# Norm weights applied as per-partition scalars after the turn instead of as rows before it, in three norms of a two-block transformer kernel

## The reference

```python
def rms_norm(x, g):
    return x * rsqrt(mean(x * x, axis=-1) + EPS) * g

# first block
h = rms_norm(x, norm_mix);  x = x + mixer(h) @ w_out
h = rms_norm(x, norm_ffn)                                   # "norm2" in the kernel
x = x + (silu(h @ w_gate) * (h @ w_up)) @ w_down
x = rms_norm(x, final_norm)
# second block
h = rms_norm_2(x, ln_mix_g_2)                               # with final_norm: "norm3"
x = x + mixer_2(h @ w_in_2) @ w_out_2
h = rms_norm_2(x, ln_ffn_g_2)                               # "norm4"
# h @ w_query -> scores -> for each token 8 heads x 16 experts of 16384:
#   x += softmax(best) * gelu(expert_u[e] . h) * expert_v[e]
```

## Time and profile before

| what | value |
|---|---|
| time, median of 3 runs | 1166.69 us (1164.12 to 1166.91) |
| the profiled execution: its own time | 1164.98 us |
| its span in the trace | 1163.2 us |
| PE busy | 1046.1 us (90%) |
| DVE busy | 791.0 us (68%) |
| ACT busy | 610.7 us (52%) |
| POOL busy | 356.0 us (31%) |
| read from HBM | 367.82 MB |
| TensorE clock granted, mean | 0.987 of full speed |

### The profile page before, as it was taken

One profiled execution on the slowest core, in us unless ns is written; L12 is line 12 of the kernel. 1 busy time (PEld: TensorE's weight loads), 2 busy tenths in 40 slices (PEclk: granted clock), 3 DMA queues, 4 the chain that ended last, 5 costly groups with the idle time before them and its releaser, 6 DMA issues.

```text
span 1163.2 us, 13131 instructions
## 1 busy us (share of the span) xinstructions
PE 1046.1 (90%) x3786; PEld 649.8 (56%) x3786; DVE 791.0 (68%) x1694; ACT 610.7 (52%) x1343; POOL 356.0 (31%) x283
## 2 busy tenths in 40 slices
PE   8999999999999999999999898878787778877777
PEld 7788888888888877885554444323232223322222
DVE  5764666755545688879686876676676667667755
ACT  7565564544445467746655555535444543544453
POOL 1000000000000000024554544556455565556442
PEclk9999999999999999999999999999899999999999
DMA  9464357775535755679999999999999999999996
GB/s 327 160 202 130 124 177 232 269 217 180 182 106 181 253 183 179 229 252 419 421 420 423 421 421 421 421 421 421 422 419 419 423 421 416 422 421 422 423 421 282
DMA packets 95760, 369.49 MB, mean 318 GB/s; under 512 B 6544, under 2 KB 30104, under 8 KB 63072
## 3 DMA queue, kind: packets, MB, share of 16 engines
q0 software_dynamic: 38464, 273.46, 56.8%
q1 hardware_dynamic: 57248, 95.45, 24.9%
HBM read 367.82 MB, written 1.06 MB: 317 GB/s over the span
## 4 chain that ended last, share of the span: by engine, by line
PE 48%; DMA 22%; DVE 10%; ACT 8%; issue 7%; POOL 4%; SPq 1%; POOLq 0%; DVEq 0%; ACTq 0%
DMA uv_ring<-in_peer_uv,expert 21%; PE gemm L1746 11%; PE gemm L1748 11%; PE gemm L1747 11%; PE gemm L2159 11%; POOL uv_ring L481 4%; DVE uv_ring L1632 2%; DVE w_both L988 1%; ACT L940 1%; ACT L912 1%; ACT diag L946 1%; PE trb L1740 1%; ACT wgt L943 1%; ACT hid_g L940 1%; DMA x_sb<-in_x 1%
## 5 line engine op out<-in xcount | busy, mean ns | idle before, releaser
L2159 PE MATMUL gemm<-uv_ring,diag 128*128 128x512 f32 x1020 | 493.6, 621 | 102.8 <-ACT diag L946 102.3
L481 POOL DMA_INDIRECT uv_ring<-in_peer_uv,expert x256 | 344.6, 1346 | 355.3 <-PE gemm L2159 195.5
L1632 DVE CUSTOM_DVE_ANT_0 uv_ring<-uv_ring,gains_xT 128x1024 f32<-128x1024 f32 x256 | 312.2, 1224 | 172.6 <-DMA uv_ring<-in_peer_uv,expert 172.4
L2159 PEld LDWEIGHTS gemm<-uv_ring,diag 128*128 128x128 f32 x1020 | 185.0, 194 | 385.1 <-ACT diag L946 225.2
L988 DVE TENSOR_TENSOR w_both<-raw,w_both 128x1024 fp32r<-128x1024 f32 (+1 forms) x184 | 192.9, 1061 | 144.1 <-ACT w_both L534 143.4
L534 ACT ACTIVATE w_both<-raw 128x1024 fp32r<-128x1024 f32 (+1 forms) x184 | 168.7, 929 | 173.2 <-PE gemm L1748 170.4
L1747 PE MATMUL gemm<-w_both,hT_hi 128*128 128x512 f32 (+1 forms) x592 | 227.4, 384 | 0.0
L940 ACT ACTIVATE hid_g<-hid,scales 128x1 f32<-128x1 f32 x256 | 75.0, 293 | 280.8 <-DVE hid L1632 279.9
L1746 PE MATMUL gemm<-w_both,hT_hi 128*128 128x512 f32 (+1 forms) x544 | 215.8, 397 | 6.0 <-DVE w_both L988 5.8
L1748 PE MATMUL gemm<-w_both,hT_lo 128*128 128x512 f32 (+1 forms) x544 | 208.9, 384 | 0.0
L1747 PEld LDWEIGHTS gemm<-w_both,hT_hi 128*128 128x128 f32 x592 | 111.5, 188 | 26.2 <-issue 6.7
(11 more groups left out here) (291 smaller groups left out, 875.6 us busy)
## 6 DMA issues: line engine op xcount, KB each, us to landing
raw<-in_w_in SPq DMA_DIRECT2D x30, 1024.0 KB, 5.1
raw<-in_w_gate SPq DMA_DIRECT2D x22, 512.0 KB, 4.0
raw<-in_w_up SPq DMA_DIRECT2D x22, 512.0 KB, 5.0
raw<-in_w_down SPq DMA_DIRECT2D x22, 512.0 KB, 3.2
raw<-in_w_out SPq DMA_DIRECT2D x8, 1024.0 KB, 5.1
uv_ring<-in_peer_uv,expert POOLq DMA_INDIRECT x258, 14.2
raw<-in_w_ret_o SPq DMA_DIRECT2D x4, 1024.0 KB, 5.4
raw<-in_peer_w_query SPq DMA_DIRECT2D x4, 1024.0 KB, 5.0
```

The lines of the kernel that those rows point to most:

```text
L481: nc.gpsimd.indirect_dma_start(out=uv_ring[k % RING][:, 0:width], out_offset=None, in_=peer_uv, in_offset=bass.IndirectOffsetOnAxis(ap=exp ...
L1632: V.tensor_tensor_reduce(out=u_row, in0=u_row, in1=xn[:, b, :], scale=1.0, scalar=0.0, op0=ALU.mult, op1=ALU.add, accum_out=hid[par][:, k: ...
L2159: last = nc.tensor.matmul(gemm[2 * b + n][:], diag[k % 4][:], uv_ring[k % RING][:, D + n * CHUNK:D + (n + 1) * CHUNK], start=(begin and k ...
```

## The change

The four `gained` products and the wait for `normed` go from norm2, norm3 and norm4. PE turns `x_sb` itself, and waits for `g_free`, which DVE's residual addition counts. The weight comes in where the bank is read: for each of the four 128 x 128 blocks of a bank, ACT's copy takes a column of `gains` as `scale`, and DVE's subtraction becomes multiply-and-subtract with the same column. The columns ride in with the first load (`gains` grows from 32 to 58 columns); `ffn_row` and `mix2_row` and their loads go; `final_row` and `peer_row` stay. The product of two weight vectors for norm3 is made on 8 columns instead of a 1024-wide row. The expert stage still needs `xn` with the weight in it: `gained(b)` now makes it in one 1024-wide product for each tile, at a place of its own in DVE's stream. Two small buffers are shared (`small`).

```diff
-    G_RET, G_BS, G_Q, G_K, G_MIX, G_COLS = 0, 8, 16, 17, 18, 32
+    G_RET, G_BS, G_Q, G_K, G_MIX, G_FFN, G_MIX2, G_FINAL, G_PEER, G_COLS = 0, 8, 16, 17, 18, 26, 34, 42, 50, 58
...
-        bn = sb("bn", [P, TB * RH, 6])
-        mv = sb("mv", [P, TB * RH, 2])
+        small = sb("small", [P, 4 * TOPK])
...
@@ POOL
-            pool.dma_start(ffn_row[:], norm_ffn[0].partition_broadcast(P)).then_inc(ffn_landed, 16)
...
-            for dst, src in ((final_row, final_norm), (mix2_row, ln_mix_g_2[0]), (gate_row, gmlp_norm_g_2[0]), (peer_row, ln_ffn_g_2[0])):
+            for dst, src in ((final_row, final_norm), (gate_row, gmlp_norm_g_2[0]), (peer_row, ln_ffn_g_2[0])):
@@ ACT, one_hi_columns, with a gain
+                    for k in range(4):
+                        ins = nc.scalar.activation(hT[0][:, 4 * half + k, b * P:(b + 1) * P], trb[t % 2][:, k * P:(k + 1) * P], ACT.Copy,
+                                                   scale=gains[:, gain + 4 * half + k:gain + 4 * half + k + 1])
+                    ins.then_inc(tr_hi, 1)
@@ ACT, norm_behind (norm2); norm3 in the same way with G_MIX2
-                hi_columns(name, (0, 1))
+                hi_columns(name, (0, 1), gain=gain)
...
-                hi_columns(name, (2, 3))
+                hi_columns(name, (2, 3), gain=gain)
@@ DVE
-            def gained(b, half, row):
-
-                cols = slice(half * CHUNK, (half + 1) * CHUNK)
-                V.tensor_tensor(xn[:, b, cols], x_sb[:, b, cols], row[:, cols], ALU.mult).then_inc(normed, 1)
+            def gained(b):
+
+                for c in (C_OUT2, C_OUT2 + 1):
+                    dve.wait_ge(g_free[2 * (c % 2) + b], c // 2 + 1)
+                me.put(V.tensor_tensor(xn[:, b, :], x_sb[:, b, :], peer_row[:], ALU.mult))
...
-            def norm_behind(name, c, row, at, scale=None):
-
-                dve.wait_ge(g_free[2 * (1 - c % 2)], (c - 1) // 2 + 1)
-                gained(0, 0, row)
+            def norm_behind(name, c, gain, at, scale=None):
+
                 residual(c, 1, (0,), scale)
-                dve.wait_ge(g_free[2 * (c % 2)], c // 2 + 1)
-                gained(0, 1, row)
                 lo_at(c + 1, quarters=(0, 1))
-                lo_columns(name, (0, 1))
-                dve.wait_ge(g_free[2 * (1 - c % 2) + 1], (c - 1) // 2 + 1)
+                lo_columns(name, (0, 1), gain=gain)
                 lo_at(c + 1, quarters=(2, 3))
-                gained(1, 0, row)
                 residual(c, 1, (1,), scale)
-                dve.wait_ge(g_free[2 * (c % 2) + 1], c // 2 + 1)
-                gained(1, 1, row)
-                lo_columns(name, (2, 3))
+                lo_columns(name, (2, 3), gain=gain)
...
-            me.link(V.tensor_tensor(mix2_row[:], mix2_row[:], final_row[:], ALU.mult))
+            me.link(V.tensor_tensor(gains[:, G_MIX2:G_MIX2 + KD], gains[:, G_MIX2:G_MIX2 + KD], gains[:, G_FINAL:G_FINAL + KD], ALU.mult))
@@ DVE, down_in
-                for n in range(2):
-                    dve.wait_ge(g_free[2 * n + b], (C_IN2 - 2 + n) // 2 + 1)
-                    gained(b, n, mix2_row)
@@ DVE, out2_row
-                dve.wait_ge(g_free[2 * (c % 2) + b], c // 2 + 1)
-                gained(b, half, peer_row)
@@ DVE, tile 0
-            one_lo_columns("norm4_10", 1, 0)
+            one_lo_columns("norm4_10", 1, 0, G_PEER)
             peer_scale(0)
+            gained(0)
             one_lo_columns("mixed_01", 0, 1)
@@ DVE, tile 1
-            one_lo_columns("norm4_01", 0, 1)
+            one_lo_columns("norm4_01", 0, 1, G_PEER)
             experts_of(0, 8, TOPK)
-            one_lo_columns("norm4_11", 1, 1)
+            gained(1)
+            one_lo_columns("norm4_11", 1, 1, G_PEER)
             variance("norm4", 1)
@@ PE, norm_columns; norm4_columns in the same way
-                    pe.wait_ge(normed, 4 * NORM[name] + n + 1)
-                    return xn[:, b, half * CHUNK:(half + 1) * CHUNK]
+                    pe.wait_ge(g_free[2 * half + b], (last_of[name] + half) // 2 + 1)
+                    return x_sb[:, b, half * CHUNK:(half + 1) * CHUNK]
```

More of the change, by code:

```diff
@@ L8, in two_block_kernel @@
 def two_block_kernel(
-    nc, x, x_t, w_in, att_sinks, w_att_o, w_ret_o, w_out, norm_ffn, w_gate, w_up, w_down,
-    final_norm, ln_mix_g_2, w_in_2, gmlp_norm_g_2, gmlp_ws_t, rel_bias_2,
+    nc, x, x_t, w_in, att_sinks, w_att_o, w_ret_o, w_out, w_gate, w_up, w_down,
+    final_norm, w_in_2, gmlp_norm_g_2, gmlp_ws_t, rel_bias_2,
     w_out_2, ln_ffn_g_2, peer_w_query_2, peer_keys_t, peer_uv, out,
@@ L224, in two_block_kernel @@
         g_soft = [sb(f"g_soft{i}", [P, TOPK]) for i in range(2)]
-        hid = [sb(f"hid{i}", [P, TOPK]) for i in range(2)]
-        hid_g = [sb(f"hid_g{i}", [P, TOPK]) for i in range(2)]
+        hid = [small[:, i * TOPK:(i + 1) * TOPK] for i in range(2)]
+        hid_g = [small[:, (2 + i) * TOPK:(3 + i) * TOPK] for i in range(2)]
         wgt = [sb(f"wgt{i}", [P, TOPK]) for i in range(2)]
@@ L703, in _ @@
                 squares(b, 0)
-            norm_behind("norm2", C_OUT + 1)
+            norm_behind("norm2", C_OUT + 1, G_FFN)
             nc.scalar.preload_act_table(ACT.Silu)
@@ L1009, in lo_columns, with one_lo_columns @@
                         ins.then_inc(tr_out[t % 2], 1)
-            def one_lo_columns(name, half, b):
+            def one_lo_columns(name, half, b, gain=None):
                 t = TR[name]
@@ L1014, in one_lo_columns @@
                 cols = slice(b * P, (b + 1) * P)
+                if gain is not None:
+                    for k in range(4):
+                        g = gain + 4 * half + k
+                        ins = V.scalar_tensor_tensor(out=hT[1][:, 4 * half + k, cols], in0=trb[t % 2][:, k * P:(k + 1) * P], scalar=gains[:, g:g + 1],
+                                                     in1=hT[0][:, 4 * half + k, cols].bitcast(f32), op0=ALU.mult, op1=ALU.subtract)
+                    ins.then_inc(tr_out[t % 2], 1)
+                    return
                 V.tensor_tensor(hT[1][:, 4 * half:4 * half + 4, cols], trb[t % 2][:].rearrange("p (k t) -> p k t", k=4),
@@ L1315, in _ @@
             lo_at(C_IN2, quarters=(0,))
-            lo_columns("norm3", (0, 1))
+            lo_columns("norm3", (0, 1), gain=G_MIX2)
             lo_at(C_IN2, quarters=(1,))
@@ L2043, in norm4_columns @@
             def norm4_columns(half, b):
-                pe.wait_ge(normed, 4 * NORM["norm4"] + 2 * b + half + 1)
-                turn(TR[f"norm4_{half}{b}"], [xn[:, b, half * CHUNK + i * P:half * CHUNK + (i + 1) * P] for i in range(4)])
+                c = C_OUT2 + half
+                pe.wait_ge(g_free[2 * (c % 2) + b], c // 2 + 1)
+                turn(TR[f"norm4_{half}{b}"], [x_sb[:, b, half * CHUNK + i * P:half * CHUNK + (i + 1) * P] for i in range(4)])
             product_at(C_IN2 + 4, by_tile=True, before={
```

48 lines of the change are left out of this document (25 added, 23 removed).

## The result

| what | before | changed |
|---|---|---|
| median | 1164.51 us (6 runs, 1163.85 to 1166.91) | 1170.97 us (6 runs, 1169.2 to 1172.3) |
| ratio, 95% interval | | 1.005 (1.0037 to 1.0063) |
| profiled execution; its span | 1164.98; 1163.2 us | 1172.3; 1170.5 us |

The change makes the kernel slower by 0.5%: 5.8 us by the ratio (4.3 to 7.3), 6.5 by the medians. The forecast had +3.2 us, and 1169.9 us for the time. Beside the experiments the kernel before had medians of 1165.6 to 1165.9 us (11 to 34 runs), which is 1.1 to 1.4 us above the 1164.51 here and speaks for the lower half of that interval.

What follows compares the result with a forecast made beforehand. DMA was taken to bound the expert stage from some 525 us, PE the work before it. Terms 1.4 + 0 + 1.0 + 0.8 + 0.04 = +3.2 us on the median 1166.69 gave 1169.9 us; range 1165.6 to 1173.4.

Steps and rivals of the forecast that it cites:

- The price of one bank: Split banks: ACT's part 0.53 us longer, DVE's 0.44 us; a bank that someone waits for is 0.97 us late.
- Norm2, +1.4: Norm2, tile 1: later banks delay roots, table load and next chunk, so PE too, by 1.4 us; tile 0 just in time.
- Norm3, 0: Norm3: what DVE saves is spent waiting for longer copies and banks, PE goes on as before; 0 us.
- rival 2: PE's clock falls too, in norm3 (+1.45), with the upper bound at gather 6 (+2.0 more): +6.7 us, 1173.4; chance 0.2.
- Norm4, tile 0, +1.0: Norm4, tile 0: PE starts `first_part(2, 0)` 0.97 us later and the chain behind moves as one; `gained(0)` is covered.
- Norm4, tile 1, +0.8: Norm4, tile 1: last bank 3.45 us later, gather 6 issued late, DMA idle 0.7 to 0.9 us.
- Alone it needs about 3.0 - 0.7 = 2.3 us of latency, its own 2.5, and some 0.5 of POOL: Gather 6, issue to landing: 5.3 us, issued at 528.6, landed at 533.9; latency taken from the 272 KB first load.
- Later gathers have more slack: Expert stage: they landed 7.5 us and more after issue, 5 needed, so the 3.45 us does not reach the end in full.
- The sum: Whole kernel: norm2 1.4, norm3 0, norm4 1.0 and 0.8, first load 0.04, together +3.2 us.
- The forecast's own case: Whole kernel: the sum as worked out, +2 to +4.5 us; chance 0.5.
- Rival 1: Norm3: split parts overlap better, PE resumes up to 1.4 us earlier; not slower, about 1167 us; chance 0.17.

Runs made afterwards that it cites:

- e_q1: Changed kernel with DVE's second quarter of weights of norm3's product moved ahead of tile 0's columns; ratio 1.0046, +5.4 us on the kernel before.
- e_remedies: Changed kernel with `gained(1)` ahead of norm4_01, norm3's quarter ahead of the columns, norm2's roots ahead of tile 1's columns, seven filling matmuls in norm3; 1.0022, +2.6 us.
- e_norm4: Kernel before with the changed kernel's layout, and the column form with the 1024-wide `gained` in norm4 alone; ratio 1.0029, +3.4 us.
- e_layout: Kernel before with only the 26 more columns in the first load and the shared small buffer, rows and `gained` kept; ratio 0.9998, -0.2 us.

## Why the prediction was half right

- **The price of one bank** was right in size: DVE 1.16 to 1.18 us behind ACT, 2.16 for two banks. The reason that I weighed for it was not: splitting is 0.39 of the 0.97 us. My estimate from the table in the Trainium skill ("VectorE: DVE Perf Modes", "The TRN2 errata") was 0.43 + 0.375 = 0.8 for a bank; plain pieces cost 0.39, so for pieces in a series the trace does not agree with that estimate. The advice there to tile at 512 elements is given for instructions that read SBUF, and these read PSUM.
- **Norm2, +1.4**: measured +1.57, by the course described (stall at the first bank, then the chain of two banks, roots, table load, next chunk; PE's row forecast for 232.3 is at 232.45 once the 1.52 us by which norm2 began late are taken off). 0.16 of it comes at tile 0, which I had at zero. Only 0.47 us came back when the roots left the series; what is left is the wait for the bank.
- **Norm3, 0**: this step failed. DVE's chain was right to 0.01 us (the next quarters start 414.75 - 408.53 = 6.22 us behind the turn, 6.21 before). What I left out was PE's own wait at the first bank, 2.00 instead of 1.13, and the clock behind it, which I had as rival 2: 4 of 5 times the low clock follows. It costs 0.8 us in the changed kernel and up to 1.1 in the same order of work (stages of 85.27 to 85.52 against 84.45), and 1.5 with the quarter moved (85.20 in `e_q1` against 83.65 in `e_remedies`); I had 1.45. Without the drop the term is +0.2. My argument against the rival, that 1.13 us of idling had cost no clock, was no evidence on 2.0.
- **Norm4, tile 0, +1.0**: +1.09, and `gained(0)` was covered (DVE still waits 1.84 us for PE behind it).
- **Norm4, tile 1, +0.8**: the mis-sized term; it is +2.76 at the issue of gather 17. DVE's part came as forecast: the last bank ends 7.78 us later than before, of which 4.13 stem from the stages ahead: 3.65, against 3.45. Gather 6 was issued 3.12 late, 0.7 less than forecast. I had added 0.4 for 12 matmuls at the low clock, and they ran at the high one (the row at 529.57 lasts 0.36 us, the one at 521.84 in the earlier trace rows 0.51). The step that failed is "Alone it needs about 3.0 - 0.7 = 2.3 us of latency, its own 2.5, and some 0.5 of POOL": 5.3 us from issue to landing. It took 7.9, and 6.0 to 8.3 over six profiles with a late gather 6; the shortest in the earlier trace rows was already 7.5. Less those 4.13 us gather 6 landed at 535.8, which is 2.6 behind the 533.2 of a queue that never stops, where I had 0.7.
- **"Later gathers have more slack"** held in this profile, since they landed at steps of 2.5 us as before, although they were issued as late as gather 6. A gather from number 8 on waits for a ring buffer that PE's row addition frees, behind DVE's dot product, and the late bank had moved that chain too: gather 9 comes 7.58 us later than before (537.15 against 529.57). In `e_norm4` a further 1.4 us was lost at gather 7.
- **One profile does not size this term.** In `e_layout`, where nothing is late, gather 6 landed 10.0 us after its issue and 4.9 behind gather 5, the same loss as in the changed kernel. Firmer is the timed +3.4 (2.3 to 4.6) of `e_norm4`: less tile 0's 1.09 it leaves 1.2 to 3.5 for tile 1, above my 0.8. Part of the 2.76 may also come back later: from the issue of gather 17 to the end it takes 612.0 us on average in the five profiles with the long start (44.1 to 44.3), and 613.4 in six with a short one (41.6 to 42.1), 1.4 more. `e_layout` has 616.2: its DMA was already late behind a short start (gather 14 landed 46.2 us behind the issue of gather 0, and 43.6 in the kernel before). What gives the 1.4 us back is open.
- **The sum**: 1.57 + 1.04 + 1.09 + 2.76 less those 1.4 is 5.1 us, inside the measured 4.3 to 7.3. The forecast's own case, which had half of the chances, ended at 4.5; what happened is rival 2 in its two halves, each smaller than I had it. The profiled execution alone has 1.57 more at 28 us, by chance. That the forecast time of 1169.9 us is only 1.1 below the measured 1170.97 is luck: it stood on a median of 1166.69 for the kernel before, which six runs put at 1164.51. The change itself costs 5.8 us by the ratio, where I had 3.2.
- **Rival 1** (DVE's relief pays) was wrong as the change stands, and right in kind: with DVE's quarter moved ahead and the clock held, norm3's stage is 0.6 us shorter than with rows in the profile. The timed runs do not show it.

## What to carry to other kernels

Moving work off an engine pays only if its order is changed with it: norm3's stage won 0.6 us in the profile, and only once DVE's next quarter stood where the removed products had been and PE did not idle. Ask of every instruction that is split or given a per-partition scalar who waits for its last piece; the extra 0.06 to 0.08 us per instruction is nothing in a stream and 1 us in a hand-over. And where an engine waits about 2 us with the low clock behind it in some executions, fill the wait before comparing small changes: here the fill gained 1.5 us, and no version of the change gained anything beyond it. A transfer that the queue no longer hides costs its whole time from issue to landing; take that from the shortest such row of the same transfer, not from a smaller load.
